# The fourth output-projection chunk of layers 0 to 3 as wide products, with two additions per tile, and a statistic one K tile later

## The reference

```python
h = rmsnorm(x, attn_norm[layer])
m = attention(h, ...)                    # one of three kinds
x = x + m @ w_o[layer]                   # the output projection, 1024 x 1024
h = rmsnorm(x, ffn_norm[layer])
x = x + conv_gated_ffn(h, w_up, conv_w, conv_b, w_down)
```

## Time and profile before, and how to read it

| what | value |
|---|---|
| median of three runs | 1476.58 us |
| the profiled execution's own time | 1474.86 us |
| span of the profiled execution | 1472.9 us |
| TensorE busy, matmuls | 1466.7 us, 10440 matmuls |
| VectorE, ScalarE, GpSimd busy | 1119.5, 926.6, 331.5 us |
| granted TensorE clock | 1.0 of full speed |

### The profile page before, as it was taken

How to read it: one execution, slowest core, us unless ns; L and a number is a source line. 1 busy time by engine, 2 the same in 40 slices (tenths; PEclk the granted TensorE clock), 3 DMA queues, 4 the chain that set the end, 5 groups by cost and what they waited for, 6 DMA issues and landing times.

```text
span 1472.9 us, 26512 instructions
## 1 busy us (share of the span) xinstructions
PE 1466.7 (100%) x10440; PEld 1357.9 (92%) x10440; DVE 1119.5 (76%) x1885; ACT 926.6 (63%) x1536; POOL 331.5 (23%) x461
## 2 busy tenths in 40 slices
PE   9999999999999999999999999999999999999998
PEld 8999989899999898989989899999898999988888
DVE  7778898565578995787899566688995688798655
ACT  7776666456756674575676456766664558566453
POOL 2104212211132222212322221023212271022100
PEclk9999999999999999999999999999999999999999
DMA  8644656444335565562565546545655464356560
GB/s 277 202 165 138 222 197 223 168 162 162 115 134 206 204 204 196 175 199 79 204 206 199 199 159 198 160 134 210 204 196 193 165 213 175 109 206 206 176 222 32
DMA packets 39687, 265.03 MB, mean 180 GB/s; under 512 B 5247, under 2 KB 5562, under 8 KB 8976
## 3 DMA queue, kind: packets, MB, share of 16 engines
q1 hardware_dynamic: 36432, 255.54, 49.9%
q0 software_dynamic: 2992, 7.79, 2.2%
q10 hardware_dynamic: 144, 0.05, 0.0%
HBM read 262.24 MB, written 1.12 MB: 179 GB/s over the span
## 4 chain that ended last, share of the span: by engine, by line
PE 98%; ACT 1%; DVE 1%; DMA 1%; issue 0%; SPq 0%; ACTq 0%
PE bank L1802 29%; PE bank L1799 14%; PE bank L1787 13%; PE bank L1788 13%; PE bank L1789 13%; PE bank L1850 6%; PE bank L1859 3%; PE bank L2034 1%; PE bank L2023 1%; PE bank L2015 1%; PE bank L2014 1%; DMA w_raw<-w_std 1%; PE bank L2394 1%; PE bank L2035 1%; PE bank L2087 0%; PE bank L2209 0%
## 5 line engine op out<-in xcount | busy, mean ns | idle before, releaser
L957 DVE TENSOR_TENSOR w_lo<-w_raw,w_hi 128x2048 fp32r<-128x2048 f32 x239 | 549.5, 2307 | 74.4 <-ACT w_hi L411 74.3
L411 ACT CAST w_hi<-w_raw 128x2048 fp32r<-128x2048 f32 x239 | 452.7, 1903 | 82.7 <-DMA w_raw<-w_std 62.4
L1802 PE MATMUL bank<-h_both,w_hi 128*128 128x512 f32 x960 | 301.5, 395 | 0.0
L1787 PE MATMUL bank<-h_both,w_hi 128*128 128x256 f32 x992 | 284.3, 287 | 0.0
L1788 PE MATMUL bank<-h_both,w_hi 128*128 128x256 f32 x992 | 280.6, 283 | 0.0
L1789 PE MATMUL bank<-h_both,w_lo 128*128 128x256 f32 x992 | 280.5, 283 | 0.0
L1802 PE MATMUL bank<-act_both,w_hi 128*128 128x512 f32 x848 | 267.4, 395 | 0.0
L1799 PEld LDWEIGHTS bank<-h_both,w_lo 128*128 128x128 f32 x960 | 179.9, 188 | 42.4 <-DVE w_lo L957 0.3
L1787 PEld LDWEIGHTS bank<-h_both,w_hi 128*128 128x128 f32 x992 | 189.9, 191 | 4.0 <-issue 2.8
L1788 PEld LDWEIGHTS bank<-h_both,w_hi 128*128 128x128 f32 x992 | 190.0, 192 | 0.4
L1789 PEld LDWEIGHTS bank<-h_both,w_lo 128*128 128x128 f32 x992 | 190.0, 192 | 0.0
(11 more groups left out here) (236 smaller groups left out, 2549.7 us busy)
## 6 DMA issues: line engine op xcount, KB each, us to landing
w_raw<-w_std SPq DMA_DIRECT2D x239, 1024.0 KB, 4.9
act_both<-vec_dram POOLq DMA_DIRECT2D x56, 128.0 KB, 3.4
w_raw<-w_std SPq DMA_DIRECT2D x3, 512.0 KB, 8.5
x<-xT SPq DMA_DIRECT2D x2, 512.0 KB, 5.5
out<-x SPq DMA_DIRECT2D x3, 256.0 KB, 2.1
w_raw<-w_std SPq DMA_DIRECT2D x2, 256.0 KB, 4.9
par<-params SPq DMA_DIRECT2D x1, 446.0 KB, 6.6
cst<-consts SPq DMA_DIRECT2D x1, 256.0 KB, 9.4
```

Source lines behind the costliest of these rows:

```text
L411: act.copy(w_hi[:, n % SLOTS, :], w_raw[:, n % RAW, :]).then_inc(hi_ready, 1)
L957: dve.tensor_tensor(w_lo[:, n % SLOTS, :], w_raw[:, n % RAW, :], w_hi[:, n % SLOTS, :].bitcast(F32), ALU.subtract).then_inc(lo_ready, 1)
L1787: pe.matmul(dst, wh, xh, start=first, stop=False, skip_group_check=shared)
L1802: done = pe.matmul(bank[:, :], weights[k][0], moving[k][1], start=False, stop=stop and k == len(weights) - 1, skip_group_check=True)
```

## The change

It does three things, in layers 0 to 3 alone:

- The fourth chunk's two tiles are computed by `wide_product`, into whole banks of 512 columns.
- `added_to_x` for tiles 6 and 7 adds the first half of the bank, waits for that addition on a new semaphore `x_half`, and adds the second half.
- The statistic in the up stage's first chunk runs after K tile 5 and not after K tile 4.

```diff
@@ added_to_x
+                        if k > 2:
+                            dve.tensor_tensor(xk, bank[:, 0:S], xk, ALU.add).then_inc(x_half, 1)
+                            dve.wait_ge(x_half, layer * 2 + k - 2)
+                            dve.tensor_tensor(xk, bank[:, S:2 * S], xk, ALU.add)\
+                               .then_inc(x_part if k == 3 else bank_free, 1)
+                            return
                         dve.tensor_tensor(xk, bank[:, 0:(b - a) * S], xk, ALU.add)\
-                           .then_inc(x_part if k == 3 else bank_free, 1)
+                           .then_inc(bank_free, 1)
@@ first_outputs
-                    elif raw not in (None, "x", "raw") and k == (5 if raw == "down3" else {"d": 2, "w": 4}.get(raw[0], 5)):
+                    elif raw not in (None, "x", "raw") and k == (5 if raw == "down3" else {"d": 2, "w": 5}.get(raw[0], 5)):
                         statistic(raw)
@@ the wo stage on TensorE
-                    for t, dst in enumerate((pj[slot][:, 0:S], val_bank[slot][:, 0:S])):
-                        done = out_part(c0 + 3, slot, t, 0, DT, dst, start=True)
+                    for t, bank in enumerate((pj[slot], val_bank[slot])):
+                        if layer < 4:
+                            done = wide_product(bank, [w_tile(weight_slot(layer, c0 + 3), k, 2 * P, t * P)
+                                                       for k in range(DT)],
+                                                [(act_hi[:, k, :], act_both[:, k, :, :].rearrange("p a b -> p (a b)"))
+                                                 for k in range(DT)], True, True)
+                            if t:
+                                done.then_inc(used, 1)
+                        else:
+                            done = out_part(c0 + 3, slot, t, 0, DT, bank[:, 0:S], start=True)
                         if t == 0:
                             done.then_inc(tile6_done, 1)
```

More of the change, by code:

```diff
@@ L186, in build @@
         x_part = sem("x_part")
+        x_half = sem("x_half")
         x_main = sem("x_main")
```

## The result

The changed kernel takes 1481.62 us (median of 7 runs, 1480.28 to 1485.48), the kernel before 1475.6 on the same chip (7 runs, 1474.22 to 1477.62): a ratio of 1.0043 (95% interval 1.0034 to 1.0052), or 6.0 us more. I had forecast 3.1 us more, and a range that ended at 1481.0. The kernel before stands 0.98 us lower in these seven runs than in the three that the forecast was made against, so the difference is the number to compare.

What follows compares the result with a forecast made beforehand. TensorE, 98% of the chain, was taken as the bound. Per layer, 0.95 us of waiting for POOL minus 0.17 gained gives 0.78, 3.1 in all: 1479.7 us on the median's scale, range 1475.4 to 1481.0.

Steps and rivals of the forecast that it cites:

- the wide products' 0.17 us a layer: Fourth chunk on TensorE: 32 matmuls replace 48, 5.59 us for 5.76, saving 0.68 us in all.
- VectorE's delay behind its first addition: Tiles 6 and 7: two dependent additions each make VectorE's first split and what follows 0.62 us late.
- The statistic in the whole change: Up stage's first chunk: run one K tile later, at 127.46, TensorE does not wait for the last addition of squares.
- The closed gap: VectorE's 0.23 us wait for ACT's cast of tile 6, which let POOL in, was to vanish after the change.
- POOL's first low part in its new place: POOL's low part of tile 1 ends at 136.55, 0.60 us after VectorE's fourth; TensorE waits 0.27 us for it.
- The step that failed: POOL's second low part ends at 137.25, before VectorE's third split; its third ends at 139.99, making TensorE wait.
- my third rival: VectorE's third split goes before POOL's second low part: 1.64 us a layer, 1483.1 us; chance 0.12.
- The 0.12 us for starting again after a wait: Added to TensorE's waits for POOL's low parts: one distance between matmuls, bounds 0 and 0.24 us.
- the upper bound of VectorE's delay: If none of the additions' 0.92 us is absorbed, the loss is 1.2 us a layer.
- this move costs TensorE nothing: Moving the statistic one K tile later, in the up stage's first chunk, was priced at no wait for TensorE.
- The first rival's condition: POOL gets in between VectorE's second split and first low part, so nothing is late: 1475.9 us; chance 0.22.

Runs made afterwards that it cites:

- Split_later: The changed kernel with two one-element memsets ahead of VectorE's third split: 1477.36 us against 1476.07 for the kernel before, ratio 1.0011.
- stat5_only: The kernel before with only the statistic moved to after K tile 5: 1483.01 us, ratio 1.0058 to the kernel before.
- gap_in_front: The changed kernel with one one-element memset between VectorE's second split and its first low part: 1477.13 us, ratio 1.0009 to the kernel before.
- gaps_between: The changed kernel with a one-element memset behind VectorE's low parts of tiles 0, 2 and 4: 1475.18 us against 1475.24 for the kernel before.
- wide_add1_stat4: The changed kernel without the second addition and with the statistic back after K tile 4: 1474.24 us against 1475.68 for the kernel before, ratio 0.999.
- wide_add1_stat5: The changed kernel without the second addition, statistic after K tile 5: 1480.62 us, ratio 1.0039 to the kernel before.
- change_stat4: The changed kernel with the statistic back after K tile 4: 1480.94 us, ratio 1.0046 to the kernel before.
- lows_all_first: The changed kernel with VectorE's second split moved behind all four of its low parts: 1497.52 us, ratio 1.014 to the kernel before.

## Why the prediction was wrong

**Right:** the wide products' 0.17 us a layer (117.22 to the first up matmul at 122.80 is 5.58 us). VectorE's delay behind its first addition: 0.61 us for 0.62. (Against the first matmul of the up stage, which the prediction's last paragraph names, it is 0.79, because that matmul comes 0.17 us earlier; the forecast's own times give 0.79 too.) The statistic in the whole change: no wait. The closed gap, and POOL's first low part in its new place 0.60 us behind VectorE's fourth. The page "SBUF — State Buffer" of the Trainium skill, in "Who interferes with whom", would have let POOL in after the second split, since whoever issues first gets the shared port pair; the row of 3.25 us at 132.96, passed over by four VectorE instructions with later starts, disagrees, as did.

**The step that failed** is this: "Its second takes the third's place and ends at 137.25. The third split runs to 139.39." I carried the old winner over to the new pair because the recorded starts stand in the same order, 0.03 us apart. They did so again (136.16 and 136.19) and the split won, in all four layers: POOL's second took 2.90 us, and TensorE waited at the low part of tile 3 (1.43 us between starts) and not at that of tile 5. That was my third rival, at 0.12, and its price was right: 1.64 us a layer, against 1.65 in layer 0. My argument against it, that both starts move together, held, and decided nothing. Split_later shows the other branch at 0.77 for the forecast's 0.78. So the sums held on both sides, and the chance was wrong: recorded starts 0.03 us apart, with one earlier outcome to go by, gave little ground to prefer a winner, so odds nearer to even were due, and 1483.1 us belonged in the range.

**Two terms of the sums.** The 0.12 us for starting again after a wait, which no row showed, is now in a row: the pair behind the wait at 139.11 takes 0.51 us for 0.40. There are two such waits a layer, and I added it once. In split_later the waits make 0.72 us for the forecast's 0.83 and the restarts 0.20 for 0.12, so its 0.77 came out right in part by compensation. And the upper bound of VectorE's delay gives 0.95 + 0.30 - 0.17 = 1.08 us a layer, where I wrote 1.2; the range does not rest on it.

**A cost I left out:** "this move costs TensorE nothing" held only under cover of the additions. I did not say what the move costs without it; stat5_only says 7.3 us, by the same lost place of POOL. The numbers for it stood in my own text: a factor ready by 129.08, against a first split that ended at 126.33 + 2.28 = 128.61 before.

**The first rival's condition** was near the truth about POOL, and not about the time: gap_in_front admits POOL behind the second split and no low part is late, but TensorE then waits for the later splits, and the time is 0.09% (0 to 0.18%) above the kernel before and not below it.

## What to carry to other kernels

Where two engines share something, price a delay by the order in which they get it, and not by its length: 0.6 us of delay here cost from nothing (gaps_between) to 1.8 us of waiting a layer (the kernel after), depending on when POOL got in. Where that order hangs on recorded starts a few hundredths of a us apart, keep both ends in the range, since two idle memsets were enough to choose between them. And when two parts of a change hide each other's delay, price each alone, because taking one back then gives nothing.

## What I had not expected of the hardware

- The recorded starts do not tell who goes first. With POOL 0.02 to 0.03 us ahead in every layer, POOL won in the kernel before and in wide_add1_stat4, VectorE in the kernel after. The outcome is the same in all four layers of each kernel. Among the kernels without added memsets that keep the order of the splits, POOL won in the two in which it had got in ahead of VectorE's fourth low part (before, wide_add1_stat4), and the split won in the four in which it had not (after, stat5_only, wide_add1_stat5, change_stat4). Whether that is what decides it is open; no run tested it.
- POOL is passed over while VectorE's subtractions follow a split without a gap (3.25 us for one of 0.74), and yet, let in once by a 0.06 us memset, it alternates with subtractions that follow each other just as closely. Why the first admission matters is open too; no run looked into it further.
- TensorE's wait of 3.6 us in layer 0 of lows_all_first went with some 7 us at half the clock, so a wait there cost more than its length: its four waits make 14.4 us, its time 21.5 us more than the kernel before. The length of a wait alone does not tell whether the clock falls: with 2.5 to 2.8 us it fell in some layers and not in others.
